# Two gate units moved into the triangular solve of a two-block decoder kernel

## What is computed

```
h = rmsnorm(x, norm_mix)
(fq, fk, fv, ff, gq, gk, gv, gb, ga, gz, sq, sk, sv, gates) = split_projection(h @ w_in)
ya = fox_attention(...)                    # softmax of scores with cumulated log forget gates
a_mat = where(strict, beta * kk * decay, 0) + eye          # 64 x 64 per chunk and head
sol = triangular_solve(a_mat, [v * beta, k * beta * exp(gc)])
yb = scan over 4 chunks: v_new = u - w @ state; o = q @ state + attn @ v_new; state = ...
yc = stick_breaking_attention(...)         # needs softplus of the scores
g = sigmoid(gates + gate_bias)
mixed = g[0] * (ya @ w_oa) + g[1] * (yb @ w_ob) + g[2] * (yc @ w_oc)
```

## Time and profile before

| | |
|---|---|
| runs of the kernel, us | 1621.75 median of 3 (1620.79 to 1622.44) |
| the profiled execution, us | 1622.98 |
| its span, us | 1621.0 |
| mean granted TensorE clock | 0.949 |
| TensorE matmuls busy | 1327.2 us, 82% of the span |
| VectorE, ScalarE busy | 608.0 us (38%), 484.0 us (30%) |

### The profile page before, as it was taken

How to read it: one execution, slowest core, us unless ns; L and a number is a source line. 1 busy time by engine, 2 the same in 40 slices (tenths; PEclk the granted TensorE clock), 3 DMA queues, 4 the chain that set the end, 5 groups by cost and what they waited for, 6 DMA issues and landing times.

```text
span 1621.0 us, 32850 instructions
## 1 busy us (share of the span) xinstructions
PE 1327.2 (82%) x14418; PEld 1048.5 (65%) x14418; DVE 608.0 (38%) x980; ACT 484.0 (30%) x811; POOL 0.2 (0%) x4
## 2 busy tenths in 40 slices
PE   9999999999999999998876586576676667558666
PEld 9999899999999999995543343343343344334333
DVE  7967556787986778641110010010110110011001
ACT  6846467556644554530000000000000000000001
POOL 0000000000000000000000000000000000000000
PEclk9999999999999999999998898898899898899889
DMA  8442034443656655799999999999999999999997
GB/s 333 160 152 98 35 134 151 173 171 132 219 207 263 252 177 193 263 343 424 429 428 429 431 428 429 431 429 427 435 429 427 429 429 433 426 429 431 428 433 310
DMA packets 42264, 517.92 MB, mean 320 GB/s; under 512 B 4816, under 2 KB 4944, under 8 KB 7248
## 3 DMA queue, kind: packets, MB, share of 16 engines
q1 hardware_dynamic: 42048, 516.71, 78.1%
q10 hardware_dynamic: 144, 0.17, 0.0%
HBM read 515.81 MB, written 1.05 MB: 319 GB/s over the span
## 4 chain that ended last, share of the span: by engine, by line
PE 50%; DMA 42%; DVE 4%; ACT 2%; issue 1%; SPq 1%; another core or an unknown queue 0%; DVEq 0%; ACTq 0%
DMA e_gu<-experts 42%; PE psum L346 11%; PE psum L347 11%; PE psum L348 11%; PE psum L986 7%; PE psum L1030 3%; DVE w_low L1696 1%; PE psum L602 1%; PE psum L1036 1%; DVE a_gdn_qk L1745 1%; DMA w_raw<-dense 0%; PE psum L962 0%; PE psum L1016 0%; SPq L2405 0%; PE psum L587 0%
## 5 line engine op out<-in xcount | busy, mean ns | idle before, releaser
L986 PE MATMUL psum<-e_gu,x_xt 128*32 128x256 f32 x3072 | 217.9, 447 | 175.2 <-DMA e_gu<-experts 175.1
L986 PEld LDWEIGHTS psum<-e_gu,x_xt 128*32 128x32 f32 x3072 | 108.3, 128 | 277.0 <-DMA e_gu<-experts 186.9
L346 PE MATMUL psum<-h_high,w_high 128*128 128x256 f32 x864 | 245.4, 284 | 0.6 <-DVE w_low L1696 0.6
L347 PE MATMUL psum<-h_low,w_high 128*128 128x256 f32 x864 | 242.7, 281 | 0.0
L348 PE MATMUL psum<-h_high,w_low 128*128 128x256 f32 x864 | 242.6, 281 | 0.0
L1696 DVE TENSOR_TENSOR w_low<-w_raw,w_high 128x2048 fp32r<-128x2048 f32 x99 | 225.7, 2288 | 28.0 <-ACT w_high L1119 20.6
L1119 ACT ACTIVATE w_high<-w_raw 128x2048 fp32r<-128x2048 f32 x99 | 189.2, 1914 | 60.2 <-PE psum L348 50.3
L2371 DVE COPY x_yb<-psum 128x256 f32<-128x256 f32 x64 | 27.2, 424 | 423.0 <-PE psum L1030 423.0
L346 PEld LDWEIGHTS psum<-h_high,w_high 128*128 128x128 f32 x864 | 162.8, 188 | 7.1 <-issue 4.7
L347 PEld LDWEIGHTS psum<-h_low,w_high 128*128 128x128 f32 x864 | 162.8, 188 | 0.1
L348 PEld LDWEIGHTS psum<-h_high,w_low 128*128 128x128 f32 x864 | 162.8, 188 | 0.0
(11 more groups left out here) (464 smaller groups left out, 2114.6 us busy)
## 6 DMA issues: line engine op xcount, KB each, us to landing
e_gu<-experts SPq DMA_DIRECT2D x44, 4096.0 KB, 52.9
w_raw<-dense SPq DMA_DIRECT2D x100, 1024.0 KB, 4.8
e_dn<-experts SPq DMA_DIRECT2D x45, 2048.0 KB, 49.4
e_dn<-experts SPq DMA_DIRECT2D x37, 1024.0 KB, 54.8
e_gu_lo<-experts SPq DMA_DIRECT2D x16, 2048.0 KB, 51.5
e_gu_hi<-experts SPq DMA_DIRECT2D x15, 2048.0 KB, 55.9
e_gu<-experts SPq DMA_DIRECT2D x8, 1024.0 KB, 6.4
e_gu<-experts SPq DMA_DIRECT2D x2, 1536.0 KB, 8.0
```

Source lines behind the costliest of these rows:

```text
L346: mm(ps, w[0], src[0], start=start, stop=False, **kw)
L347: mm(ps, w[0], src[1], start=False, stop=False, **kw)
L986: last = mm(half(psum[32 * s:32 * s + 32, GU_BANK[j % 2], 0:256], P), X["xt"][:, k, CAP * j:CAP * (j + 1)], expert_gu(j, k)[:, :, s * P:(s ...
```

## The change

Two gate units, ga00 and ga01, are run in the fourth and fifth level of the solve (lv 3 and 4), between the product and the update, and no longer at the start of branch a. The order of the units, and so of the banks and of the weight ring, stays. Head 3's exponentials on ScalarE move from the end of the third level to behind the copies of the fourth. An empty step in each of the three lists of forget attention steps puts the later ones half a level back. VectorE makes the low part of oa_0 in the fourth level and no longer behind the solve.

```
@@ TensorE
-                            lambda: fox_scores(3), lambda: fox_turn(2),
+                            lambda: fox_scores(3), lambda: fox_turn(2), lambda: None,
                             lambda: (fox_turn(3), pv("fpv", 2, "fox_pT", A["pt"], A["fox_v"])),
                             lambda: pv("fpv", 3, "fox_pT", A["pt"], A["fox_v"])])
...
                 elif lv < 3:
                     unit_tok(f"sv{lv - 1}")
+                elif lv < 5:
+                    unit(f"ga0{lv - 3}")
                 between()
                 solve_tu(lv, 0)
...
                     for p in range(2):
-                        gate(b, hf, p)
+                        if b != "a" or hf:
+                            gate(b, hf, p)
                         step()
@@ ScalarE
-                          lambda: softmax_exp(A["s"], A["st"], "fox", 2, FSP),
+                          lambda: softmax_exp(A["s"], A["st"], "fox", 2, FSP), lambda: None,
                           lambda: softmax_exp(A["s"], A["st"], "fox", 3, FSP),
@@ VectorE
-                          lambda: (fout(1), fmax(2)), lambda: (fnorm(2), fmax(3)), lambda: fnorm(3), lambda: fout(2),
+                          lambda: (fout(1), fmax(2)), lambda: (fnorm(2), fmax(3)), lambda: None, lambda: fnorm(3), lambda: fout(2),
...
-                if lv < 3:
-                    lows(("sv0", "sv1", "ga01")[lv])
+                if lv < 4:
+                    lows(("sv0", "sv1", "ga01", "oa_0")[lv])
...
-            lows("oa_0")
             sb_keep(0); state(0); lows("ga10"); lows("ga11"); sb_keep(1); mix("a", 0, 0); vnew(1); mix("a", 0, 1); sb_masked(0)
```

## The result

The changed kernel takes 1626.06 us (median of 8 runs, 1625.39 to 1627.8), the kernel before 1621.05 (8 runs, 1620.29 to 1622.44). The ratio is 1.0031, with a 95% interval from 1.0022 to 1.0039: the change makes the kernel 5.0 us slower. The profiled execution took 1626.51 us.

A forecast was written before the change was run, and what follows sets the result against it. TensorE was taken to bound half the span, expert loads 42%, delays near the solve counting one to one. Terms: -3.78 + 5.8 + 1.7 = +3.7 us on the median 1621.75, giving 1625.5 us, range 1622.6 to 1627.8.

The forecast's parts named there:

- The cover is moved from behind the solve into it, and a wait opens at L625: At chunk 1's product with the state, TensorE waits about 5.1 us for VectorE's state, behind ScalarE's logarithm; start at 212.0.
- The last product of the solve: L617 ends near 199.8, the solve ending 7.91 us later: two units add 11.69 us, 3.78 us is gained.
- The first output: Chunk 0's first output, just behind the solve, waits for VectorE's copy of the solution: 0.7 us lost.
- The clock behind L625: After the wait at L625 TensorE runs some 3.4 us near half clock, costing 1.7 us (0.5 to 2.9).
- No second stall: After L625 TensorE has no further wait before 260 us; at 700 us everything comes 3.7 us later.
- The solve's wait goes: A unit covers the 1.97 us wait before the fourth level's update (L602), gaining 2.13 us; moved exponentials add nothing.
- 1.65 us of clock, counted as a gain in the solve: The fourth level's update, 5.30 us at partly half clock, would take 3.65 us like the fifth's.
- Rival (a): The wait at L625 opens but costs little clock: +2.0 to +2.9 us, 1624.2 us; 17 in 100.
- Rival (c): State ready when TensorE reaches L625, ScalarE's chain ending 5.1 us sooner: -3.1 us, 1618.6 us; 7 in 100.
- Rival (b): Half clock lasts 5.70 us behind L625, or a second wait opens: +4.6 to +6.3 us, 1627.2 us; 12 in 100.
- (d): A projection bank or low weights come late for units in the solve: -1 to +1 us, 1621.8; 4 in 100.
- The Trainium skill's 2.7 us for a change of table set: ScalarE's table load before the sigmoids takes 2.7 us, not 1.28: total 1626.9 us; 2 in 100.

The follow-up runs named there:

- Experiment 3: The changed kernel with only ga00 in the solve and ga01 back behind the first scores: 1619.45 us, ratio 0.999 to the kernel before.
- experiment 4: The changed kernel with VectorE's state copies in front of sb_keep(0), which waits for the logarithm: 1626.45 us, ratio 1.0035 to the kernel before.
- experiment 6: The changed kernel with ScalarE's first logarithm before its first sigmoids, and VectorE's state copies, head 0's masks and first mixes before the second head's part: 1620.33 us, ratio 0.9993.
- experiment 5: The changed kernel with 20 products of the identity with itself on TensorE in front of the wait at L625: 1623.82 us, ratio 1.0015 to the kernel before.
- experiment 2: The changed kernel without its empty steps, head 3's exponentials at their old place, both units in the solve: 1625.91 us, ratio 1.0031 to the kernel before.
- experiment 1: The kernel before with only the three empty steps, head 3's exponentials behind the fourth level's copies, no unit moved: 1619.06 us against 1621.32, ratio 0.9986.

## Why the prediction was right, and where a size was off

The forecast was 1625.5 us and slower; 1626.06 was measured, ratio 1.0031. That the two times lie 0.6 us apart is in part luck. The forecast was a shift of 3.7 us on a median of 3 runs, 1621.75; the median of 8 was 1621.05, and the shift 5.0. The spans of the two profiled executions do differ by 3.7 us (1621.0 and 1624.7), but 3.1 of them stand at the milestone and the rest is scatter behind it. By its steps:

- **The cover is moved from behind the solve into it, and a wait opens at L625.** Shown: 4.84 us for the state, where 5.1 were forecast, start at 211.62 (212.0). Experiment 3 shows that one unit less moved closes it, experiment 4 that another order on VectorE closes it (and opens others), and experiment 6 that both orders rewritten leave none of 0.6 us or more.
- **The last product of the solve.** Forecast to end near 199.8. It starts at 198.49 and the rows before it are 0.9 us apart, so 199.4. The units take 5.76 and 5.77 us (168.73 to 174.49, 180.09 to 185.86), 0.16 less together than was forecast, and the solve gains 4.0 us, not 3.78; each of the two updates takes 3.57 us where 3.65 was counted.
- **The first output** waits 0.55 us for VectorE's copy, forecast 0.7.
- **The clock behind L625** falls, for 3.5 us at 0.51; 1.5 us by experiment 5, forecast 1.7.
- **No second stall.** Right: no further wait up to 330 us, and the shift is 3.1 us at the sums of head 0 and at the milestone, for 3.7 forecast at 700 us.
- **The solve's wait goes.** Right, but the reason I leaned on was half of it. I wrote that the unit gives the gain and that the moved exponentials give nothing on top. That holds with the unit in place (experiment 2), but the units were not needed: the exponentials alone give 3.1 of the 4.0 us (experiment 1), and 2.3 us on the whole kernel.
- **The term that was mis-sized: 1.65 us of clock, counted as a gain in the solve.** It was read from one profile, in which the clock had fallen, and set against the median of the runs. In 3 of 5 profiles of the kernel before there is no such loss to win back, and the fourth level's update takes 3.68 us there (171.21 to 174.89 in the second). With the gain of the solve at 2.13 us the same sum gives 3.7 + 1.65 = 5.3 us, and with the fall counted in 2 of 5 executions some 4.7 (an estimate); measured were 5.0. I had noted that the profiled execution lay 1.2 us above the median and had not asked why.

Rival (a), a wait that costs little clock, is ruled out for the profiled executions by the windows. Rival (c) would have needed ScalarE to be 5 us sooner. In experiment 6 its logarithm starts 4.5 us sooner and the wait is gone, but there VectorE's state copies don't stand behind the logarithm any more, so that doesn't test (c) by itself. Rival (b) did not show in the change, but something like it did in experiment 4. Neither low part nor bank was late in the solve, as (d) needed. The Trainium skill's 2.7 us for a change of table set ("ScalarE: Activation LUTs", Rules for kernel authors) isn't met by this trace: the load in the open was 1.28 us again, and the whole switch, from the end of the copy before it (200.18) to the sigmoid (201.65), 1.47.

What stays open is the spread of the expert part. From the milestone to the end of the span it takes 927.9 to 929.3 us in the five profiles of before, and I tried nothing there; this scatter, 1.4 us, is about as large as the clock's.

## What to carry to other kernels

A matmul unit that fills a wait is taken from somewhere: ask what it covered there, and for whom the next engine works in the meantime, before moving it. If an engine waits because a copy stands behind another wait in a third engine's written order, swap those two first; that cost nothing here and gave more than moving 11 us of work. And when one profiled execution lies above its median, look for a fall of the clock behind a short wait before counting it as a gain.

## What the runs showed of the hardware that I had not expected

The same kernel with the same 1.97 us wait had TensorE at half clock (the 1.2 GHz level) behind it in 2 of 5 executions and at full clock in 3. Behind a wait of 2.25 us the clock stayed low for some 7 us in one execution and 10 us in another (experiment 4), longer than the 3.5 us behind the wait of 4.84 us. And with TensorE kept busy through the 4.9 us wait, by products that nobody reads, the clock stayed at 1 and the median was 2.2 us below the changed kernel's (experiment 5).
